# A transformer block on one Trainium2 core: the second RMS norm's root and reciprocal taken by token, four values a partition

## Chip, cores and metric

One core of a Trainium2 chip runs the whole program in one launch. The core has five engines, each with its own instruction stream: TensorE (PE in the profile, its weight loads PEld), VectorE (DVE), ScalarE (ACT), GpSimd (POOL) and SyncE (SP), which here only issues transfers. They wait for each other through semaphores. The metric is the device time of one execution in microseconds; lower is better.

## The reference, cut to what matters

Everything is float32, with 512 tokens and 1024 channels.

```python
def rms_norm(x, g):
    x32 = x.astype(jnp.float32)
    y = x32 * lax.rsqrt(jnp.mean(x32 * x32, axis=-1, keepdims=True) + EPS)
    return (y * g.astype(jnp.float32)).astype(x.dtype)
...
        mod = (cond @ w_ada[l] + b_ada[l])[:, None, :]
        shift1, scale1, gate1, shift2, scale2, gate2 = jnp.split(mod, N_MOD, axis=-1)
        n1 = rms_norm(h, g_norm1[l]) * (1 + scale1) + shift1
        z = n1 @ w_in[l]
        ...
        h = h + gate1 * (merged @ w_out[l])
        n2 = rms_norm(h, g_norm2[l]) * (1 + scale2) + shift2
        h = h + gate2 * peer(n2, w_pq[l], sub_keys[l], peer_u[l], peer_v[l])
    return rms_norm(h, g_final)
```

The change concerns `n2`, the second `rms_norm`. `peer` begins with `n2 @ w_pq`, scores against keys, and picks the best 16 of each of 8 heads for every token; its dense part runs over 16384 expert rows.

## The kernel before

Up to `peer`, activations are stored transposed: a channel is a partition and the 512 tokens lie along the row, in KT = 8 tiles of 128 channels. `hT` is the residual stream, `nT` the normed one. The program is written out by hand, engine by engine; the order in the code is the order on the engine, and semaphores tie them together.

The work around the second norm, in order:

- TensorE multiplies `w_out` with the merged branches, 8 output tiles of 24 products of 128x512 (L784).
- For each output tile d, VectorE adds it, gated, into `hT` (L1561), ScalarE squares it (`square`, L1121) into one of two buffers `sq`, and VectorE adds the squares of the tiles together in `std` (`sum_square`, L1555). `std` and `rstd` are the two halves of the tile `stats`.
- The modulation vector `mod` (six parts of 1024) is made alongside: VectorE forms `macc[q]` (L1341) and TensorE sums each over its 128 partitions by 8 products with one column each (`modulation(q)`, L621). These narrow products have a 128x128 weight load apiece. Parts 3, 4 and 5 are summed behind the `w_out` products; part 3 and 4 are shift and scale of this norm, part 5 is the last gate.
- TensorE adds `std` over the channels by one product with a matrix of ones (L793), so that every partition holds all 512 sums. ScalarE takes the root (`root`, L983), which needs a table load, VectorE the reciprocal of 128x512 values (L1319) and multiplies it into the 8 tiles (L1326), and ScalarE applies scale and shift (`modulate`, L989).
- TensorE then multiplies `n2` with `w_pq` (`pq_tile`, L630): 16 output tiles of 8 products, tile k of the first waits for `n_ready` k. Its products, as all of its type here, are in float32, which the profile shows as two records each with 128x128 weights: one product is "x2".
- Scores of a head (L825) go through ScalarE (L1166) to VectorE, which sorts out the best 16.

Since TensorE takes its instructions in order, the first `pq_tile` cannot begin before `modulation(4)` and `modulation(5)` are through.

Of the kernel before, what the change touches and what calls it, by code (L numbers as in the profile page):

```python
# [7 lines left out]
P = 128  # L8
D = 1024
T = 512  # L10
KT = D // P
TB = T // P
CT = 4
# [61 lines left out]
N_RMS1 = 0  # L75
# [5 lines left out]
N_RMS2 = N_WOUT + KT  # L81
N_PQ = N_RMS2 + 1
N_LIST = N_PQ + 2 * PH
BANKS = 4

def build(nc, stream, wada, skT, xT, cols, rows, biasd, identd, puT, pu, pv, gmat, hsave, out):
    f32, f32r, i32, u32 = mybir.dt.float32, mybir.dt.float32r, mybir.dt.int32, mybir.dt.uint32
    ALU, ACT, AX = mybir.AluOpType, mybir.ActivationFunctionType, mybir.AxisListType
    NEG = -3.0e38  # L90

    with ExitStack() as ctx:
# [3 lines left out]
        def sem(name):  # L96
            return ctx.enter_context(nc.semaphore(name))
# [15 lines left out]
        hT = big[:, 8 * D:12 * D].rearrange("p (k t) -> p k t", k=KT)  # L113
        nT = big[:, 12 * D:16 * D].rearrange("p (k t) -> p k t", k=KT)
# [4 lines left out]
        bias = low[:, 0:2 * D].rearrange("p (h k) -> p h k", k=KEYS)  # L119
# [3 lines left out]
        ident = sb("ident", [P, P])  # L123
        ones = sb("ones", [P, P])
        eps = sb("eps", [P, 1])
# [4 lines left out]
        std, rstd = stats[:, 0:T], stats[:, T:2 * T]  # L130
# [12 lines left out]
        sq = att[:, 6 * T:8 * T].rearrange("p (a t) -> p a t", a=2)  # L143
# [14 lines left out]
        zeros = sb("zeros", [P, P])  # L158
        ssum = sb("ssum", [P, TB])
        sstd = sb("sstd", [P, TB])  # L160
# [140 lines left out]
        sq_ready, sq_used = sem("sq_ready"), sem("sq_used")  # L301
        sum_ready, y_summed, lsum_ready = sem("sum_ready"), sem("y_summed"), sem("lsum_ready")
        scaled = sem("scaled")
        n_ready = sem("n_ready")
        gate_done, gate_taken = sem("gate_done"), sem("gate_taken")
        gates_ready = sem("gates_ready")
# [44 lines left out]
        def freed(eng, n):  # L351

            eng.wait_ge(bank_free[n % BANKS], n // BANKS + 1)
# [237 lines left out]
        def _(pe):  # L591
            def bank(n):

                if n >= BANKS:
                    pe.wait_ge(bank_free[n % BANKS], n // BANKS)
                return ps[:, n % BANKS, :]
# [20 lines left out]
            def modulation(q):  # L617

                pe.wait_ge(macc_ready, q + 1)
                for c in range(KT):  # L620
                    mm = nc.tensor.matmul((MOD if q < 2 else MOD2 if q == 2 else MOD3 if q < 5 else MOD5)[:, q * KT + c:q * KT + c + 1],  # L621
                                          macc[q][:, c * P:(c + 1) * P], ones[:, 0:1], start=(q >= 2),
                                          stop=(q >= 2 or (q == 1 and c == KT - 1)))
                return mm
# [130 lines left out]
            o = bank(N_LN)  # L755
# [33 lines left out]

            pe.wait_ge(attn_merged, KT)  # L790
            modulation(3)
            pe.wait_ge(sum_ready, KT - 1)
            nc.tensor.matmul(bank(N_RMS2), ones[:, :], std, start=True, stop=True).then_inc(tile_done, 1)  # L793
            modulation(4).then_inc(mod_done, 1)
            modulation(5).then_inc(mod_done, 1)

            def transposed(i, src, b, half):
# [170 lines left out]
        def _(act):  # L968
# [12 lines left out]
            def root(n, count):  # L981
                act.wait_ge(tile_done, n + 1)
                f(std, ps[:, n % BANKS, :], ACT.Sqrt, bias=eps[:, 0:1], scale=1.0 / count  # L983
                  ).then_inc(bank_free[n % BANKS], 1)
# [131 lines left out]
            def square(k):  # L1116

                freed(act, N_WOUT + k)
                if k >= 2:
                    act.wait_ge(sum_ready, max(k - 2, 1))  # L1120
                f(sq[:, k % 2, :], hT[:, k, :], ACT.Square).then_inc(sq_ready, 1)  # L1121
# [2 lines left out]
                wout_round(d)  # L1124
                square(d - 2)

            for k in range(KT - 2, KT):
                square(k)
            root(N_RMS2, D)
            act.wait_ge(mod_ready, 4)  # L1130
            modulate()

# [170 lines left out]
        def _(dve):  # L1303
# [3 lines left out]
            def step(ins):  # L1307

                count[0] += 1
                ins.then_inc(dve_step, 1)  # L1310

            def settled():

                dve.wait_ge(dve_step, count[0])

            def scale_rows(stage, between=None):
                n = N_RMS2 if stage else N_RMS1
                freed(dve, n)
                step(v.reciprocal(rstd, std))  # L1319
                settled()  # L1320
                for k in range(KT):
                    if stage and k == 0:
                        dve.wait_ge(gate_done, 2 * KT)
                    if stage and between:
                        between(k)
                    v.tensor_tensor(nT[:, k, :], hT[:, k, :], rstd, ALU.mult).then_inc(scaled, 1)  # L1326
                    if between and not stage:
                        between(k)

            def take_mod(src, c0, c1):  # L1330
                return v.tensor_tensor(mod[:, c0:c1], src[:, c0:c1], b_ada[:, c0:c1], ALU.add)
# [78 lines left out]
            for i in range(KT):  # L1410
                chunk(i)
            dve.wait_ge(x_here, 16)
            scale_rows(0, early_chunk)
            w_rest(0)
            w_rest(1)
            first_coefficients()
# [133 lines left out]
            def sum_square(k):  # L1550

                dve.wait_ge(sq_ready, KT + CT + k + 1)
                if k > 1:
                    dve.wait_ge(sum_ready, k - 1)
                v.tensor_tensor(std, sq[:, 0, :] if k == 1 else std, sq[:, k % 2, :], ALU.add).then_inc(sum_ready, 1)  # L1555

            dve.wait_ge(mod_ready, 2)
            for d in range(KT):
# [8 lines left out]
                    chunk(5 * KT - 2 + 2 * d + 1)  # L1567
                if d >= 2:
                    sum_square(d - 1)
            sum_square(KT - 1)  # L1570
            for k in range(4, KT):
                freed(dve, N_WOUT + k)
            def second_coefficients(k):
                if k == 0:
# [2 lines left out]
                    dve.wait_ge(mod_ready, 3)  # L1577
                    v.scalar_tensor_tensor(coef[:, 1, :], mod[:, 4 * KT:5 * KT], 1.0, g2, ALU.add, ALU.mult
                                           ).then_inc(mod_ready, 1)
            scale_rows(1, second_coefficients)  # L1580
            dve.wait_ge(mod_done, 4)
            step(take_mod(MOD5, 5 * KT, 6 * KT))
            settled()
# [356 lines left out]
```

## Time and profile before

| | |
|---|---|
| time, median of 3 runs | 1626.87 us (1626.63 to 1627.47) |
| time of the profiled execution | 1631.68 us |
| its span in the trace | 1629.9 us |
| mean granted clock of TensorE | 0.985 of 2.4 GHz |
| PE busy | 1589.4 us, 98% |
| DVE busy | 1375.0 us, 84% |
| ACT busy | 636.2 us, 39% |
| chain that ended last | PE 81%, DVE 12%, DMA 3% |

### The profile page before, as it was taken

Reading aid. Unit: us, or ns where it says so; the run is one execution under the profiler, and the core shown is the slowest. Engines: PE = TensorE matmul, PEld = TensorE weight load, DVE = VectorE, ACT = ScalarE, POOL = GpSimd, SP = SyncE. Lnnn points to the kernel's source line nnn. Section 1 sums busy time; section 2 is a strip of 40 time slices with the busy share of each in tenths; the row PEclk is TensorE's granted clock in tenths of the full one; section 3 lists DMA queues with packets and bytes.
Section 4 is the critical chain, followed back from the end, with each engine's and each line's share of the span. In section 5 each row is a group of like instructions: output and inputs, shape, how many; then the busy total and the mean of one; then the engine's idle time right before and its main releaser. Section 6 shows DMA issues by size and latency. Waiting matters only on the chain.

```text
span 1629.9 us, 23615 instructions
## 1 busy us (share of the span) xinstructions
PE 1589.4 (98%) x7933; PEld 1314.9 (81%) x7933; DVE 1375.0 (84%) x2751; ACT 636.2 (39%) x952; POOL 560.0 (34%) x479
## 2 busy tenths in 40 slices
PE   6999999999999999999999999999999999999997
PEld 4887764675556799988988889898889898898886
DVE  6787877764999999977989898988988888988886
ACT  3334654241112566663333333333333333333333
POOL 0000000011555300005545455554545565656520
PEclk7999999989999999999999999999999999999999
DMA  9432215641212255589999999999999999999981
GB/s 366 177 119 78 78 52 182 229 157 65 91 71 84 73 196 212 187 293 357 385 372 358 371 361 368 372 358 370 355 349 347 334 362 363 347 346 355 355 296 61
DMA packets 144459, 417.87 MB, mean 256 GB/s; under 512 B 11520, under 2 KB 56576, under 8 KB 138624
## 3 DMA queue, kind: packets, MB, share of 16 engines
q1 hardware_dynamic: 96128, 247.01, 42.2%
q0 software_dynamic: 47104, 167.83, 27.1%
q10 hardware_dynamic: 1152, 2.10, 0.3%
q8 instruction: 40, 0.66, 0.2%
q14 instruction: 35, 0.29, 0.1%
HBM read 389.59 MB, written 27.26 MB: 256 GB/s over the span
## 4 chain that ended last, share of the span: by engine, by line
PE 81%; DVE 12%; DMA 3%; issue 2%; ACT 1%; SPq 0%; DVEq 0%; ACTq 0%
PE ps L919 30%; PE ps L857 26%; PE ps L639 11%; PE ps L630 6%; PE ps L907 3%; PE ps L784 3%; DMA big<-pv 1%; DVE low L1764 1%; DVE att L1632 1%; DMA big<-wada 1%; DVE att L1643 1%; DVE big L1630 1%; DVE big L1648 1%; DVE low L1609 1%; DVE low L1757 1%
## 5 line engine op out<-in xcount | busy, mean ns | idle before, releaser
L919 PE MATMUL ps<-Vs,As 128*128 128x512 f32 x2286 | 537.1, 390 | 2.7 <-DVE As L1796 2.7
L919 PEld LDWEIGHTS ps<-Vs,As 128*128 128x128 f32 x2286 | 426.3, 188 | 87.5 <-DVE As L1796 3.0
L857 PE MATMUL ps<-xs,Us 128*128 128x352 f32 x2832 | 472.2, 322 | 2.7 <-DVE Us L1776 2.2
L857 PEld LDWEIGHTS ps<-xs,Us 128*128 128x128 f32 x2832 | 453.9, 188 | 15.8 <-DVE Us L1751 3.6
L568 POOL DMA_INDIRECT big<-pv,islot x160 | 234.3, 1465 | 167.5 <-DVE low L1835 81.8
L1275 ACT ACTIVATE att<-ps 128x352 f32<-128x352 f32 x96 | 44.7, 466 | 413.5 <-PE ps L857 413.5
L1793 DVE TENSOR_TENSOR Vs<-big,Vs 128x1024 fp32r<-128x1024 f32 x127 | 155.3, 1223 | 35.3 <-ACT Vs L1281 35.2
L630 PE MATMUL ps<-big 128*128 128x512 f32 (+1 forms) x416 | 162.8, 550 | 0.0
L1835 DVE SCALAR_TENSOR_TENSOR low<-big,act_w,low 128x1024 f32<-128x1024 f32 x128 | 157.3, 1279 | 0.0
L1281 ACT ACTIVATE Vs<-big 128x1024 fp32r<-128x1024 f32 x127 | 134.0, 1055 | 53.5 <-PE ps L919 42.4
L630 PEld LDWEIGHTS ps<-big 128*128 128x128 f32 x416 | 79.5, 194 | 74.9 <-issue 58.5
L568 POOL DMA_INDIRECT low<-pu,islot x80 | 101.4, 1268 | 101.8 <-DVE colv L1805 85.7
L516 POOL TENSOR_TENSOR xs<-big,xs 128x352 fp32r<-128x352 f32 x8 | 7.1, 928 | 361.0 <-ACT xs L1137 361.0
L1154 ACT ACTIVATE Us<-big 128x1024 fp32r<-128x1024 f32 x118 | 124.0, 1050 | 12.9 <-DMA big<-puT 12.8
L568 POOL DMA_INDIRECT big<-pu,islot x80 | 102.6, 1282 | 67.7 <-DVE colv L1805 36.9
L1790 DVE TENSOR_TENSOR att<-att 128x352 f32<-128x352 f32 x96 | 50.3, 523 | 88.8 <-ACT att L1275 87.5
L1776 DVE TENSOR_TENSOR Us<-big,Us 128x1024 fp32r<-128x1024 f32 x95 | 116.0, 1221 | 8.4 <-ACT Us L1154 8.4
L639 PE MATMUL ps<-ahi,whi 128*128 128x512 f32 x240 | 97.6, 407 | 3.3 <-DVE alo L1355 3.3
L1764 DVE TENSOR_SCALAR low<-iotan,att 128x128 f32<-128x128 f32 x352 | 97.7, 341 | 0.0
L559 POOL COPY islot<-eidx 128x8 int32 (+1 forms) x40 | 27.0, 675 | 203.1 <-DMA gmat<-big 170.5
L639 PE MATMUL ps<-alo,whi 128*128 128x512 f32 x240 | 95.3, 397 | 0.0
L639 PE MATMUL ps<-ahi,wlo 128*128 128x512 f32 x240 | 95.1, 396 | 0.0
(233 smaller groups left out, 2035.4 us busy)
## 6 DMA issues: line engine op xcount, KB each, us to landing
big<-puT SPq DMA_DIRECT2D x128, 512.0 KB, 6.0
big<-pv SPq DMA_DIRECT2D x64, 1024.0 KB, 11.2
big<-stream SPq DMA_DIRECT2D x31, 1024.0 KB, 4.9
gmat<-big SPq DMA_DIRECT2D x11, 2048.0 KB, 7.2
att<-gmat SPq DMA_DIRECT2D x31, 704.0 KB, 11.8
low<-wada SPq DMA_DIRECT2D x28, 512.0 KB, 5.2
work<-wada SPq DMA_DIRECT2D x12, 512.0 KB, 5.2
big<-wada SPq DMA_DIRECT2D x8, 512.0 KB, 13.5
```

The source lines that it names most:

```text
L568: nc.gpsimd.indirect_dma_start(out=places[r % ROWBUF], out_offset=None, in_=table, in_offset=bass.IndirectOffsetOnAxis(ap=islot[:, half, s ...
L630: mm = nc.tensor.matmul(o, lhs(k), rhs(k), start=(k == 0), stop=(k == count - 1))
L639: mm = nc.tensor.matmul(o, w, a[:, k, :], start=(k == 0 and w is hi and a is ahi), stop=(k == KT - 1 and w is lo))
L857: mm = nc.tensor.matmul(ps[:, 6 + e, 0:ET], a, xs[:, b, k, XTOK:DT], start=(k == 0 and a is hi and b == 0), stop=(k == KT - 1 and a is lo))
L919: mm = nc.tensor.matmul(ps[:, 2 * b + half, :], a, v_parts[:, w, half * T:(half + 1) * T], start=(opens and a is hi and w == 0), stop=(las ...
L1154: f(Us[:, e, 0, :], uraw[:, e, :], ACT.Copy).then_inc(uhi_ready, 1)
L1281: f(Vl[:, 0, :] if last and d == BODY - 1 else Vs[:, d % 2, 0, :], vraw[:, d // 2 % 2, d % 2, :], ACT.Copy).then_inc(vhi_ready, 1)
L1764: mm = v.tensor_scalar(ohi[:, 4 * c + t, :], iotan[:, :], lists[:, 0, tok:tok + 1], lists[:, 2, tok:tok + 1], ALU.is_equal, ALU.mult)
L1776: v.tensor_tensor(Us[:, e, 1, :], uraw[:, e, :], Us[:, e, 0, :].bitcast(f32), ALU.subtract).then_inc(ulo_ready, 1)
L1790: v.tensor_tensor(ga, ga, graw[:, (d // GRUN + 1) % 2, :, d % GRUN, :], ALU.mult).then_inc(a_ready, 1)
L1793: v.tensor_tensor(V[:, 1, :], vraw[:, d // 2 % 2, d % 2, :], V[:, 0, :].bitcast(f32), ALU.subtract).then_inc(vlo_ready, 1)
L1835: i = v.scalar_tensor_tensor(acc[:, r % 2, :], src, w, acc[:, r % 2, :], ALU.mult, ALU.add)
```

## The change

Three things are different.

1. VectorE no longer adds the last squares into `std` (`sum_square(KT - 1)` is gone). TensorE sums per token instead: the data become the weights and a column of ones the moving side, so that the sum of a token lands in the partition of that token. Four products take `std`, which holds tiles 0 to 6, four take `sq` of the last tile, one more with zeros opens the bank.
2. ScalarE takes the root of 128x4 values, after a root of `eps` alone that stands ahead of the last square, and VectorE the reciprocal of 128x4.
3. VectorE multiplies the identity matrix by those four columns into `rstd` (128x512, one diagonal per block of 128 tokens), TensorE multiplies it by ones into PSUM bank 4, and VectorE's eight multiplications read that bank instead of `rstd` in SBUF. This product stands between `modulation(4)` and `modulation(5)`.

```diff
@@ TensorE
             modulation(3)
-            pe.wait_ge(sum_ready, KT - 1)
-            nc.tensor.matmul(bank(N_RMS2), ones[:, :], std, start=True, stop=True).then_inc(tile_done, 1)
+            o = bank(N_RMS2)
+            nc.tensor.matmul(o[:, 0:TB], zeros[:, :], ones[:, 0:TB], start=True, stop=False)
+            pe.wait_ge(sum_ready, KT - 2)
+            for b in range(TB):
+                nc.tensor.matmul(o[:, b:b + 1], std[:, b * P:(b + 1) * P], ones[:, 0:1], start=False, stop=False)
+            pe.wait_ge(sq_ready, KT + CT + KT)
+            for b in range(TB):
+                mm = nc.tensor.matmul(o[:, b:b + 1], sq[:, (KT - 1) % 2, b * P:(b + 1) * P], ones[:, 0:1], start=False,
+                                      stop=(b == TB - 1))
+            mm.then_inc(tile_done, 1)
             modulation(4).then_inc(mod_done, 1)
+            pe.wait_ge(root_spread, 1)
+            nc.tensor.matmul(ps[:, 4, :], ones[:, :], rstd, start=True, stop=True).then_inc(root_done, 1)
             modulation(5).then_inc(mod_done, 1)
@@ ScalarE
-            for k in range(KT - 2, KT):
-                square(k)
-            root(N_RMS2, D)
+            square(KT - 2)
+            f(sstd[:, 0:1], eps[:, 0:1], ACT.Sqrt)
+            square(KT - 1)
+            act.wait_ge(tile_done, N_RMS2 + 1)
+            f(sstd[:, :], ps[:, N_RMS2 % BANKS, 0:TB], ACT.Sqrt, bias=eps[:, 0:1], scale=1.0 / D
+              ).then_inc(bank_free[N_RMS2 % BANKS], 1)
@@ VectorE
+            def scale_tokens(between):
+
+                freed(dve, N_RMS2)
+                step(v.reciprocal(srstd[:, :], sstd[:, :]))
+                settled()
+                v.tensor_tensor(rstd.rearrange("p (b t) -> p b t", b=TB), ident[:, :].unsqueeze(1).broadcast_to([P, TB, P]),
+                                srstd[:, :].unsqueeze(2).broadcast_to([P, TB, P]), ALU.mult).then_inc(root_spread, 1)
+                dve.wait_ge(gate_done, 2 * KT)
+                between(0)
+                dve.wait_ge(root_done, 1)
+                for k in range(KT):
+                    v.tensor_tensor(nT[:, k, :], hT[:, k, :], ps[:, 4, :], ALU.mult).then_inc(scaled, 1)
...
-            sum_square(KT - 1)
...
-            scale_rows(1, second_coefficients)
+            scale_tokens(second_coefficients)
```

TensorE's instructions behind the `w_out` products, before (the operands are named out<-in; `work` holds `macc[3]` to `macc[5]`, `stats` is `std`):

```order
L621 MATMUL ps<-ones,work 128x1 x7
L793 MATMUL ps<-stats,ones 128x512 [waits bank_free1,sum_ready]
L621 MATMUL ps<-ones,work 128x1 [waits macc_ready]
L621 MATMUL ps<-ones,work 128x1 x7
L621 MATMUL ps<-ones,work 128x1 [waits macc_ready]
L621 MATMUL ps<-ones,work 128x1 x7
L630 MATMUL ps<-big 128x512 [waits n_ready,bank_free2,w_here3]
L630 MATMUL ps<-big 128x512 [waits n_ready] x7
```

The same place in the changed kernel, whose lines are numbered anew (L631 is the `w_pq` product, `att` holds `sq`, `stats` is `std` in L797 and `rstd` in L805):

```order
L622 MATMUL ps<-ones,work 128x1 x7
L794 MATMUL ps<-ones,zeros 128x4 [waits bank_free1]
L797 MATMUL ps<-ones,stats 128x1 [waits sum_ready]
L797 MATMUL ps<-ones,stats 128x1 x3
L800 MATMUL ps<-ones,att 128x1 [waits sq_ready]
L800 MATMUL ps<-ones,att 128x1 x3
L622 MATMUL ps<-ones,work 128x1 [waits macc_ready]
L622 MATMUL ps<-ones,work 128x1 x7
L805 MATMUL ps<-stats,ones 128x512 [waits root_spread]
L622 MATMUL ps<-ones,work 128x1 [waits macc_ready]
L622 MATMUL ps<-ones,work 128x1 x7
L631 MATMUL ps<-big 128x512 [waits n_ready,bank_free2,w_here3]
```

One product of 512 columns ahead of `modulation(4)` has given way to one of four columns and eight of one, and a product of 512 columns now stands ahead of `modulation(5)`.

VectorE from the last tile's `hT` on, before:

```order
L1561 SCALAR_TENSOR_TENSOR big<-ps,mod,big 128x512 [waits tile_done]
L1555 TENSOR_TENSOR stats<-stats,att 128x512 [waits sum_ready,sq_ready] x2
L1319 RECIPROCAL stats<-stats 128x512 [waits bank_free0,bank_free3,bank_free1,bank_free2]
L1331 TENSOR_TENSOR mod<-ps,colv 128x16 [waits mod_done,gate_done,dve_step]
L1578 SCALAR_TENSOR_TENSOR coef<-mod,colv 128x8 [waits mod_ready]
L1326 TENSOR_TENSOR big<-big,stats 128x512 x8
L1331 TENSOR_TENSOR mod<-ps,colv 128x8 [waits mod_done]
```

And in the changed kernel:

```order
L1582 SCALAR_TENSOR_TENSOR big<-ps,mod,big 128x512 [waits tile_done]
L1576 TENSOR_TENSOR stats<-stats,att 128x512 [waits sum_ready,sq_ready]
L1341 RECIPROCAL srstd<-sstd 128x4 [waits bank_free0,bank_free3,bank_free1,bank_free2]
L1343 TENSOR_TENSOR stats<-ident,srstd 128x512 [waits dve_step]
L1352 TENSOR_TENSOR mod<-ps,colv 128x16 [waits mod_done,gate_done]
L1598 SCALAR_TENSOR_TENSOR coef<-mod,colv 128x8 [waits mod_ready]
L1349 TENSOR_TENSOR big<-big,ps 128x512 [waits root_done]
L1349 TENSOR_TENSOR big<-big,ps 128x512 x7
L1352 TENSOR_TENSOR mod<-ps,colv 128x8 [waits mod_done]
```

The last sum of squares and the wide reciprocal are gone, a 128x4 reciprocal and a 128x512 product with the identity have come, and the eight multiplications now stand behind `root_done` and read `ps`.

## Rows read from the trace of the kernel before

**Rows 1.** The page: span, granted clock of TensorE in 40 slices.

```profile
span 1629.9 us, 23615 instructions
...
PEclk7999999989999999999999999999999999999999
```

**Rows 2.** Chain that ended last, 340 to 400 us: start, us, what.

```profile
349.76 1.26 PE ps L793 x2
351.02 6.62 PE ps L621 x32
357.64 15.50 PE ps L630 x32
...
397.75 1.80 PE ps L825 x16
```

**Rows 3.** Timeline around the norm: start, us, engine, line, operation.

```profile
347.36 1.84 PE L621 MATMUL ps<-ones,work 128*128 128x1 f32 x16
...
348.23 1.48 DVE L1555 TENSOR_TENSOR stats<-stats,att 128x512 f32<-128x512 f32 x2
...
348.99 1.28 ACT L983 ACT_TABLE_LOAD   x1
...
350.81 6.83 PE L621 MATMUL ps<-ones,work 128*128 128x1 f32 x32
...
351.06 0.69 ACT L983 ACTIVATE stats<-ps,eps 128x512 f32<-128x512 f32 x1 [0.79 <-PE ps L793]
351.88 3.35 DVE L1319 RECIPROCAL stats<-stats 128x512 f32<-128x512 f32 x1 [2.18 <-ACT stats L983]
...
355.56 4.90 DVE L1326 TENSOR_TENSOR big<-big,stats 128x512 f32<-128x512 f32 x8
356.34 5.75 ACT L989 ACTIVATE big<-big,mod,coef 128x512 f32<-128x512 f32 x8 [4.59 <-DVE big L1326]
...
357.50 15.64 PE L630 MATMUL ps<-big 128*128 128x512 f32 x32
358.50 0.34 PEld L630 LDWEIGHTS ps<-big 128*128 128x128 f32 x1 [0.52 <-issue]
359.35 0.34 PEld L630 LDWEIGHTS ps<-big 128*128 128x128 f32 x1 [0.52 <-issue]
```

**Rows 4.** Windows: us, busy of PE, PEld, DVE, ACT, POOL; clock, DMA.

```profile
349.00:350.00 1.00, 0.44 (x3) 0.36 (x3) 0.69 (x1) 1.00 (x1) 0.00 (x0) 1.00 0.57 238
350.00:351.00 1.00, 1.00 (x4) 0.42 (x3) 0.00 (x0) 0.28 (x1) 0.00 (x0) 0.80 0.00 0
351.00:352.00 1.00, 1.00 (x8) 1.00 (x6) 0.12 (x1) 0.69 (x1) 0.00 (x0) 0.50 0.00 0
...
360.00:361.00 1.00, 1.00 (x3) 0.38 (x2) 0.96 (x5) 1.00 (x2) 0.00 (x0) 0.58 0.58 90
361.00:362.00 1.00, 1.00 (x4) 0.52 (x3) 1.00 (x7) 1.00 (x3) 0.00 (x0) 1.00 0.76 270
```

**Rows 5.** VectorE, groups by line and form: busy, mean ns.

```profile
L1757 DVE TENSOR_TENSOR low<-iotan,att 128x512 f32<-128x512 f32 x88 | 60.2, 684 | 0.7 <-PE ps L907 0.5 <-PEq L901 0.2
...
L1477 DVE TENSOR_TENSOR gates<-ps,gates 128x512 f32<-128x512 f32 x8 | 5.5, 689 | 10.3 <-PE ps L630 10.3
```

**Rows 6.** Instructions on the tile sstd: ns min/median/max, starts.

```profile
L1261 ACT ACTIVATE sstd<-ssum,eps x4: 294/294/295, 1613.4 to 1625.0; 128x1 f32<-128x1 f32 x4
L1850 DVE RECIPROCAL srstd<-sstd x4: 156/160/164, 1613.8 to 1625.4; 128x1 f32<-128x1 f32 x4
```

**Rows 7.** TensorE timeline and windows where two other wide streams begin.

```profile
40.92 0.76 PE L639 MATMUL ps<-ahi,whi 128*128 128x512 f32 x1 [3.35 <-DVE alo L1355]
...
142.86 0.79 PE L639 MATMUL ps<-ahi,whi 128*128 128x512 f32 x1
...
43.60:47.00 3.40, 3.40 (x10) 2.67 (x9) 3.30 (x7) 1.68 (x3) 0.00 (x0) 0.53 0.58 237
...
142.50:146.00 3.50, 3.50 (x12) 2.65 (x11) 3.42 (x7) 1.73 (x8) 0.00 (x0) 0.53 0.01 2
```

More of the change, by code:

```diff
@@ L303, in build @@
         scaled = sem("scaled")
+        root_spread, root_done = sem("root_spread"), sem("root_done")
         n_ready = sem("n_ready")
@@ L1314, in settled, with scale_rows @@
                 dve.wait_ge(dve_step, count[0])
-            def scale_rows(stage, between=None):
-                n = N_RMS2 if stage else N_RMS1
-                freed(dve, n)
+            def scale_rows(between):
+                freed(dve, N_RMS1)
                 step(v.reciprocal(rstd, std))
@@ L1321, in scale_rows @@
                 for k in range(KT):
[L1322 to L1325, printed above, removed]
                     v.tensor_tensor(nT[:, k, :], hT[:, k, :], rstd, ALU.mult).then_inc(scaled, 1)
-                    if between and not stage:
-                        between(k)
+                    between(k)
+            def scale_tokens(between):
[9 more added lines that the diff above has]
+                    v.tensor_tensor(nT[:, k, :], hT[:, k, :], ps[:, 4, :], ALU.mult).then_inc(scaled, 1)
             def take_mod(src, c0, c1):
@@ L1412, in _ @@
             dve.wait_ge(x_here, 16)
-            scale_rows(0, early_chunk)
+            scale_rows(early_chunk)
             w_rest(0)
```

## The prediction

> **What bounds the kernel now.** I began with the page, to see how long the span is and where TensorE's clock is below full [rows 1]. Then I took the chain that ended last around the second norm, to see who hands over to whom [rows 2], the timeline of the same stretch, to see what runs beside that chain [rows 3], and windows of 1 us, for the clock [rows 4].
>
> The chain comes out of the last sum over squares into TensorE's product with ones at 349.76 and then stays on TensorE: 32 records of L621, which are `modulation(4)` and `modulation(5)`, to 357.64, then the `w_pq` products, and so on to the scores of the second head at 397.75 [rows 2]. It does not go through the wide reciprocal. That one runs from 351.88 for 3.35 us, VectorE's multiplications begin at 355.56, and ScalarE's `modulate` at 356.34 [rows 3]. ScalarE does 8 tiles in 5.75 us, so 0.72 each, and the first normed tile is ready at 357.06. TensorE begins `w_pq` at 357.50 [rows 3]. So TensorE's own queue ends last, 0.4 us behind the norm: the norm's detour over ScalarE and VectorE lies almost wholly beside narrow products. A shorter detour alone can bring 0.4 us and no more.
>
> The second thing to see is the clock. It reads 1.00 up to 350, 0.80 in the next microsecond and 0.50 after that; the windows between 352 and 360 read 0.50 too, 360 to 361 reads 0.58, and then it is 1.00 [rows 4]. With two levels, 0.80 means a fall at 350.6 and 0.58 a rise at 360.84. It is the fall from 2.4 to 1.2 GHz, and TensorE had done narrow products since 347.36, with one wide one (512 columns) in between. It came back 3.3 us after the wide `w_pq` products began. From 357.50 to 360.84 these ran at half rate, which loses 1.67 us of work.
>
> **What the narrow and wide products cost.** At 2.4 GHz the 8 products of `modulation(3)` take 1.84 us [rows 3]; the last one's tail is in that, so I take 0.22 each. At 1.2 GHz 16 of them go from 350.81 to 357.50, 0.42 each [rows 3]. A wide float32 product is two records; at 1.2 GHz its weight loads start 0.85 us apart (358.50, 359.35), so it takes 1.70 us [rows 3], and half of that, 0.85, at 2.4 GHz.
>
> **The change, on TensorE.** Before, from the end of `modulation(3)` on: a wait, one wide product from 349.76 on, 16 narrow ones. After, behind `modulation(3)`, whose 8 products end at 347.36 + 8 x 0.22 = 349.1:
>
> - Nine narrow products (one with zeros, four on `std`, four on the last square). Their inputs are there: the first of the two last sums at 348.23 + 1.48/2 = 348.97, the last square also at about 349.0, since the table load that follows it starts at 348.99 [rows 3]. If the fall of the clock stays at 350.6, 6.8 of them run at 0.22 and 2.2 at 0.42: end at 351.5.
> - `modulation(4)`, 8 x 0.42: 354.9.
> - The spreading product, wide, at 1.2 GHz: 1.70, to 356.6. It waits for `root_spread`; see below.
> - `modulation(5)`, 3.36: 360.0.
>
> So `w_pq` can start at 360.0, against 357.50: **+2.5 us**. The removed wide product (0.85 at full clock) and the removed wait of 0.7 (349.1 to 349.76) are in this; what is added is nine narrow products, and the wide one comes back at half clock.
>
> **The change, off TensorE.** The narrow sums land some 0.3 us behind their last product, 351.8: the removed product took 1.26 us to its end [rows 2] where 0.85 is its streaming, which bounds such a tail by 0.4. A root of 128x4 is not in the trace; a root of 128x1 takes 0.294 and a reciprocal of 128x1 0.16 [rows 6]. The upper bounds are the 128x512 forms, 0.69 and 3.35 [rows 3]; four values are close to one, so I take 0.3 and 0.16, to 352.3 with 0.1 for the hand-overs. The product with the identity reads two broadcast operands; the nearest row is L1757, the same shape with broadcasts, 0.684 [rows 5]. It is ready at 353.1, and TensorE asks for it at 354.9: `modulation(4)` hides it with 1.8 us to spare. Only with the reciprocal at its upper bound would the wait show, with 1.4 us. The early table load falls into ScalarE's wait for the last tile of `hT`. It was hidden before as well: it ended at 350.27 and the root began at 351.06 [rows 3]. Its gain is nothing.
>
> From the spreading product on: it lands at 356.6 + 0.4 = 357.0. VectorE's first multiplication now reads PSUM; the nearest row, L1477, shows 0.689 for a tile with one operand in PSUM, against 4.90/8 = 0.61 for SBUF alone [rows 3, 5]. With ScalarE's 0.72 the first normed tile is ready at 358.4. TensorE is free at 360.0, so this is hidden with 1.6 us to spare; cover for it is `modulation(5)`. Tiles then come every 0.72, and TensorE needs 0.85 or 1.70 for one. VectorE's eight multiplications end 0.6 us later relative to their start, with nothing waiting. Bank 4 is read until about 362.6 and next written by the scores, behind both `pq_tile`s of the first head, more than 12 us later. What VectorE does next, diagonals for the last gate, is wanted by TensorE only behind these 16 products.
>
> **The clock behind it.** `w_pq` loses half of the time from its start to the rise. Rises in this trace: 3.3 us after the wide products began (here), 5.9 (40.92 to 46.8) and 2.9 (142.86 to 145.8); the last two by means of 0.53 over 3.4 and 3.5 us, which put 0.2 us at full clock at the window's end [rows 7]. So the loss behind 360.0 is 1.45 to 2.95 us, against 1.67 before. The whole is +2.5 - 0.2 = +2.3 to +2.5 + 1.3 = **+3.8 us**. At the same TensorE work, everything to the second head's scores follows one for one [rows 2].
>
> The profiled execution took 1631.68 us, its span 1629.9, and is 4.8 us over the median of the runs (1626.87). So its clock need not be that of the timed runs in every place, and I take a value near the lower end, +2.6, because the fall may also come later there: 1626.9 + 2.6 = **1629.5 us**, which is +0.16%. I count a difference within 0.2%, 3.25 us, as none, since measurements of this kernel hardly tell it from no change.
>
> **The rivals.**
>
> *The spreading product counts as the start of the wide stream.* It starts at 354.9, so the clock would be back 2.9 to 5.9 us later, at 357.8 to 360.8. Earliest: `modulation(5)` runs 1.2 us at half rate (2.9 products) and the rest, 5.1 x 0.22 = 1.1, at full: `w_pq` from 358.9 at full clock. The kernel before, with its loss, is as if it had started at 357.50 + 1.67 = 359.17. That is -0.3 us. Latest: start 360.0, loss 0.4, so +1.2. For it: it is the only wide work ahead of `w_pq`. Against it: the product at 349.76 did not keep the clock from falling at 350.6, and eight narrow ones follow the spreading product. Time 1626.6 to 1628.1.
>
> *The clock does not fall at all (the faster side).* In the changed kernel TensorE has no idle time from the `w_out` products to `w_pq`, where before it waited 0.7 us. At full clock: nine narrow to 351.1, `modulation(4)` 352.9, the spread just ready then (352.7 by the steps above), 353.7, `modulation(5)` 355.5; the first tile at 353.7 + 0.4 + 0.69 + 0.72 = 355.5 as well. Against 359.17 this is -3.7 us, 1623.2. It decides only if the clock holds past all of it: each microsecond longer at 2.4 GHz gives half a microsecond, so +2.6 is used up when the fall comes 5 us later, at 355.8. Against it: from 351 to 357.5 TensorE is busy without a gap, with narrow products, and the granted clock stays at 0.50 [rows 4]. The Trainium skill, "TensorE: Matmul & The Clock Gate", Part 1, has the clock gated by how busy the engine has been, idle being what throttles it; taken as the profile's busy time this would speak for this rival and for 1623.2. By the rows narrow products do not hold the clock up.
>
> *The rise comes late and the start too.* If the rise takes 5 us or more, as at 40.92, the loss is over 2.5 and the sum over +3.3: slower by more than 0.2%, 1630.2 to 1630.7. The rows allow 2.9 to 5.9; about a third of it lies there.
>
> *The wait for `root_spread` or for the multiplications from PSUM ends last.* With 1.4 us shown for the first it would be +4 and 1630.9; the rows give it 1.8 and 1.6 us of cover, so it needs prices far from the nearest rows.
>
> **How the numbers follow.** TensorE's queue with the clock falling where it does now: 0.70, of which 0.22 beyond +3.25. The spreading product helps the clock: 0.15. No fall: 0.07. A new wait, or a later low stretch that grows: 0.08, slower. Faster by over 0.2%: 0.07. Within 0.2%: 0.48 + 0.15 = 0.63. Slower: 0.22 + 0.08 = 0.30. The range leaves out the two cases with 0.07 and 0.08 and keeps the others: -0.3 to +3.8, a little wider for the timed runs, 1626.3 to 1631.2.
>
> **What would show it in the profile after.** Right: nine narrow products end near 351.5, the fall stays near 350.6, VectorE's reciprocal takes under 0.3 us and ends by 352.5, TensorE has no wait ahead of the spreading product, that one takes 1.7 us, `w_pq` starts near 360.0 and the rise follows 2.9 to 5.9 us later; the chain stays on TensorE. Wrong: a granted clock of 1.00 between 351 and 357 (then faster), `w_pq` that begins behind ScalarE instead of behind L622, or an idle TensorE ahead of L805.

## The result and the profile after

The changed kernel takes 1631.25 us at the median of 17 runs (1627.89 to 1634.50), the kernel before 1627.47 in the same measurement (17 runs, 1625.05 to 1629.54). The ratio is 1.0018 with a 95% interval of 1.0011 to 1.0026: some 2.9 us slower, clear of no change. It lies inside the 0.2% that I had set as a bound, though the interval reaches past it. (The two medians alone are 3.8 us apart; the ratio is not that of the medians.) In two later measurements, each on its own chip with experiments beside it, the changed kernel came out at 1.0008 (0.9995 to 1.0020) and 1.0011 (1.0002 to 1.0020), so +1.3 and +1.8 us. The three intervals overlap: slower is clear in two of them, each leaves the size open by a bit over 1 us to either side.

The profiled execution of the changed kernel is, of all things, shorter than that of before: its span is 1628.2 us against 1629.9 [rows 1]. The page's row of clock tenths says where to look for the reason: its first slice differs from before, ahead of anything that the change touches.

```profile
span 1628.2 us, 23650 instructions
...
PEclk8999999989999999999999999999999999999999
```

TensorE's granted clock is at 0.50 for 50.5 us of the span of before and for 43.7 us of this one. Around the norm it is low for longer now (below); the difference the other way lies in stretches far from the change (one near 142 us [rows 7] and one near 542 us are in the profile of before and not in this one). So one span says nothing about a change of 3 us. What can be compared is the stretch itself, counted from the start of `modulation(3)`: 347.36 before [rows 3], 345.45 here.

The timeline of the stretch after the change (start, us, engine, line, operation, idle time before):

```profile
345.45 1.84 PE L622 MATMUL ps<-ones,work 128*128 128x1 f32 x16
...
347.15 0.36 PE L794 MATMUL ps<-ones,zeros 128*128 128x4 f32 x2
...
347.38 1.03 PE L797 MATMUL ps<-ones,stats 128*128 128x1 f32 x8
...
348.27 1.32 PE L800 MATMUL ps<-ones,att 128*128 128x1 f32 x8
...
349.45 3.55 PE L622 MATMUL ps<-ones,work 128*128 128x1 f32 x16
349.63 0.26 ACT L1142 ACTIVATE sstd<-ps,eps 128x4 f32<-128x4 f32 x1 [2.56 <-PE ps L800]
350.02 0.18 DVE L1341 RECIPROCAL srstd<-sstd 128x4 f32<-128x4 f32 x1 [3.02 <-ACT sstd L1142]
350.23 0.69 DVE L1343 TENSOR_TENSOR stats<-ident,srstd 128x512 f32<-128x512 f32 x1
...
352.86 2.06 PE L805 MATMUL ps<-stats,ones 128*128 128x512 f32 x2
...
354.71 3.41 PE L622 MATMUL ps<-ones,work 128*128 128x1 f32 x16
...
354.96 4.87 DVE L1349 TENSOR_TENSOR big<-big,ps 128x512 f32<-128x512 f32 x8 [1.47 <-PE ps L805]
355.74 5.75 ACT L1000 ACTIVATE big<-big,mod,coef 128x512 f32<-128x512 f32 x8 [5.85 <-DVE big L1349]
...
357.98 8.50 PE L631 MATMUL ps<-big 128*128 128x512 f32 x14
```

The diagonal is written by 350.92 and TensorE takes it up at 352.86, behind `modulation(4)`. ScalarE has its first tile at 355.74 + 0.72 = 356.46, while TensorE comes to `w_pq` at 357.98, behind `modulation(5)`. The chain that ended last says the same (start, us, what):

```profile
347.52 0.89 PE ps L797 x8
348.41 1.18 PE ps L800 x8
349.59 3.41 PE ps L622 x16
353.00 1.92 PE ps L805 x2
354.92 3.20 PE ps L622 x16
358.12 16.08 PE ps L631 x32
```

Before, it came through VectorE's last sum into L793, which the row ahead of [rows 2] shows:

```profile
349.01 0.70 DVE stats L1555
```

Now, between 340 and 400 us, it never leaves TensorE. The windows show the clock (its value stands behind the five busy columns, as in [rows 4]):

```profile
348.00:349.00 1.00, 1.00 (x10) 1.00 (x10) 0.00 (x0) 0.00 (x0) 0.00 (x0) 0.93 0.00 0
349.00:350.00 1.00, 1.00 (x6) 1.00 (x6) 0.00 (x0) 0.26 (x1) 0.00 (x0) 0.50 0.00 0
...
362.00:363.00 1.00, 1.00 (x3) 0.37 (x2) 0.00 (x0) 1.00 (x4) 1.00 (x2) 0.74 0.97 410
```

It falls at 348.86 and is back at 362.5, 13.65 us later; before it was low from 350.61 to 360.85, 10.24 us.

VectorE's first maximum over the scores of the first head is a point that all versions share, behind the low clock. Here, then before:

```profile
385.80 1.64 DVE L1641 MAX8 att<-big 128x8 f32<-128x128 f32 x8 [24.12 <-ACT big L1180]
...
384.73 1.65 DVE L1621 MAX8 att<-big 128x8 f32<-128x128 f32 x8 [22.43 <-ACT big L1166]
```

That is 40.35 and 37.37 us behind the start of `modulation(3)`: **3.0 us later**. I use this distance, "to the first scores", for the experiments as well, and beside it the distance to the first `w_pq` product.

The difference is still there at the dense part, though it doesn't look so at first. Its first product starts 203.90 us behind `modulation(3)` in the changed kernel and 202.69 before, only 1.2 us apart:

```profile
542.38 4.90 PE L631 MATMUL ps<-big 128*128 128x352 f32 x16
...
549.35 2.95 PE L868 MATMUL ps<-xs,Us 128*128 128x352 f32 x17
...
541.39 6.59 PE L630 MATMUL ps<-big 128*128 128x352 f32 x16
...
550.05 2.15 PE L857 MATMUL ps<-xs,Us 128*128 128x352 f32 x12
```

The first two rows are of the changed kernel. The profile of before had the clock at 0.50 for 3.41 us from 541.75 on, and the same 16 records took 1.7 us longer there. Without that it is 2.9 us. Such a stretch stands there in the second trace of the changed kernel too and not in the third, so it doesn't go with the change.

### The profile page after: what moved, and what is told of

It is laid out like the page before. It is cut to its first block, busy times and chain, and to the rows that moved or that the text cites. A ratio compares the mean times of both kernels' runs of the same rounds, so it can differ in the third digit from the quotient of the medians.

```text
span 1628.2 us, 23650 instructions
## 1 busy us (share of the span) xinstructions
PE 1588.6 (98%) x7951; PEld 1314.4 (81%) x7951; DVE 1371.6 (84%) x2751; ACT 636.4 (39%) x953; POOL 563.4 (35%) x479
## 4 chain that ended last, share of the span: by engine, by line
PE 81%; DVE 12%; DMA 3%; issue 2%; ACT 1%; SPq 0%; DVEq 0%; ACTq 0%
PE ps L930 30%; PE ps L868 26%; PE ps L640 10%; PE ps L631 6%; PE ps L918 3%; PE ps L785 3%; DMA big<-pv 1%; DVE low L1784 1%; DVE att L1652 1%; DMA big<-wada 1%; DVE att L1663 1%; DVE big L1650 1%; DVE big L1668 1%; DVE low L1629 1%; DVE low L1777 1%
## 5 line engine op out<-in xcount | busy, mean ns | idle before, releaser
L631 PE MATMUL ps<-big 128*128 128x512 f32 (+1 forms) x416 | 161.7, 547 | 0.0
L631 PEld LDWEIGHTS ps<-big 128*128 128x128 f32 x416 | 78.9, 192 | 74.4 <-issue 57.8
## 6 DMA issues: line engine op xcount, KB each, us to landing
att<-gmat SPq DMA_DIRECT2D x31, 704.0 KB, 13.3
```

What stands on the lines that cost most here:

```text
L631: mm = nc.tensor.matmul(o, lhs(k), rhs(k), start=(k == 0), stop=(k == count - 1))
```

## The experiments

Two theories went in. Q: TensorE's queue got longer and the clock comes back later for it. N: the norm's own way over ScalarE and VectorE sets the start of `w_pq`. The last column is the timed ratio to the kernel before within one measurement; the distances, in us behind the start of `modulation(3)`, come from one trace each.

| kernel | to `w_pq` | clock at 0.50, from and to | to the first scores | ratio, 95% |
|---|---|---|---|---|
| before | 10.14 | 3.25, 13.49 | 37.37 | 1 |
| changed | 12.53 | 3.41, 17.06 | 40.35 | 1.0018 (1.0011 to 1.0026) |
| changed, 2nd time | 13.26 | 2.60, 16.26 | 40.31 | 1.0008 (0.9995 to 1.0020) |
| changed, 3rd time | 12.66 | 3.28, 16.93 | 40.35 | 1.0011 (1.0002 to 1.0020) |
| changed, 64-column modulations | 11.46 | 3.18, 10.01 | 37.02 | 0.9996 (0.9983 to 1.0009) |
| before, 64-column modulations | 9.94 | 10.34, 13.75 | 37.20 | 0.9992 (0.9980 to 1.0004) |
| the same, 2nd time | 9.95 | 10.34, 13.76 | 37.21 | 0.9999 (0.9989 to 1.0009) |
| before, last square by a second wide product | 9.94 | 8.78, 15.61 | 38.32 | 0.9992 (0.9981 to 1.0004) |
| changed, `modulation(5)` behind a `w_pq` tile | 12.21 | 2.35, 16.00 | 41.44 | 1.0026 (1.0014 to 1.0037) |
| changed, all squares added on VectorE | 11.81 | 3.35, 17.01 | 39.96 | 1.0018 (1.0007 to 1.0029) |
| before, nine one-column products more | 12.35 | 3.61, 17.26 | 40.36 | 1.0017 (1.0007 to 1.0028) |
| before, nine 64-column products more | 12.69 | 3.23, 16.88 | 40.34 | 1.0015 (1.0003 to 1.0026) |
| changed, 64 columns in all narrow products | 8.59 | none | 34.16 | 0.9980 (0.9970 to 0.9991) |
| the same, 2nd time | 8.60 | none | 34.16 | 0.9975 (0.9963 to 0.9988) |

**The changed kernel again.** No edit. Expected:

> The changed kernel once more, beside the experiments of this group. Theory Q (TensorE's queue got longer, and the clock comes back later for it): from the start of modulation(3) to the start of w_pq 12.5 us, as in its first trace, and 2 to 4 us over the kernel before in time. Theory N (the norm's own way over ScalarE and VectorE sets the start of w_pq) has w_pq begin right behind a tile of ScalarE's modulate.

> The changed kernel again, beside the two below on one chip. Over the kernel before by 0.1 to 0.25%.

The first scores came where Q has them, the time did not: 2 to 4 us over the kernel before was expected and +1.3 us measured (interval -0.8 to +3.3). In the third measurement it is +0.11%, at the low end of the expected 0.1 to 0.25%. The distances to the first scores repeat within 0.04 us. The distance to `w_pq` does not (12.5 to 13.3), since the fall of the clock comes anywhere from 2.6 to 3.4 us behind the start of `modulation(3)`; what an early fall costs ahead of `w_pq` an earlier rise gives back inside it. The medians were 1631.26 and 1630.42 us.

**64 columns in the modulations of the changed kernel.** The weights and their order stay; each product writes 64 equal columns, and VectorE reads one of them (parts 3 and 4 in two additions where it was one).

```diff
+        WIDE = {q: ps[:, b, 0:64 * KT].rearrange("p (c w) -> p c w", w=64) for q, b in ((3, 7), (4, 6), (5, 5))}
...
+                if q >= 3:
+                    for c in range(KT):
+                        mm = nc.tensor.matmul(WIDE[q][:, c, :], macc[q][:, c * P:(c + 1) * P], ones[:, 0:64],
+                                              start=True, stop=True)
+                    return mm
```

> The changed kernel, with the products of modulation(3) to modulation(5) made 64 columns wide instead of one (the same weights, all columns alike, one of them read). Work on the weights is the same. Theory Q with the clock as part of the cause: if wider products hold the granted clock at 1.00, the nine narrow products, two modulations and the spreading product take 2.0 + 1.8 + 0.85 + 1.8 us, w_pq starts 8.2 to 8.6 us behind modulation(3) and at full clock, 4 to 6 us faster than the changed kernel and 1 to 3 us faster than the kernel before. Rival (the clock follows something else, such as waits): clock falls all the same, time within 1 us of the changed kernel. Theory N: no gain, since the norm's way is not touched.

The clock still fell, at 347.84 with the nine one-column products, but it was back at 354.67, ahead of `w_pq`, instead of inside it. The rows of the timeline and of a window:

```profile
348.87 3.65 PE L624 MATMUL ps<-ones,work 128*128 128x64 f32 x16
...
354.13 2.15 PE L624 MATMUL ps<-ones,work 128*128 128x64 f32 x16
...
354.00:355.00 1.00, 1.00 (x7) 0.86 (x6) 0.62 (x2) 0.00 (x0) 0.00 (x0) 0.66 0.00 0
```

`modulation(4)` still takes 3.65 us and `modulation(5)` 2.15. The first scores come 3.3 us earlier than in the changed kernel, 37.02, and 0.35 us earlier than before. The timed ratio went from 1.0008 to 0.9996, which is 2 us where I had put down 4 to 6; the two intervals overlap. Against the kernel before, where I had put down 1 to 3 us, there is no measurable gain. The expectation was too high, since I had the clock held throughout. N has no place for the earlier scores at all.

**The same in the kernel before.**

> The kernel before with the same 64-column modulations. Theory Q: if the clock holds, modulation(4) and (5) end early and the norm's way with the wide reciprocal becomes the bound: w_pq starts about 9.7 us behind modulation(3)'s start (10.1 before), at full clock instead of half, so 1.5 to 2.5 us faster than before, less than the changed kernel gains. If the clock falls during the wait for the norm instead, then no gain. Theory N: the gain is equal in both kernels or none.

> The kernel before with 64-column modulations, again. 0.9985 to 1.0000 of the kernel before: the wide reciprocal bounds it once the modulations are quick.

Here both modulations end early (32 records in 3.68 us, where it was 6.83 [rows 3]), and for once `w_pq` waits for ScalarE:

```profile
348.61 3.68 PE L623 MATMUL ps<-ones,work 128*128 128x64 f32 x32
...
355.19 15.67 PE L636 MATMUL ps<-big 128*128 128x512 f32 x32 [2.90 <-ACT big L995]
```

It begins only 0.2 us sooner than before, and 0.4 us behind its start, after the wait of 2.90 us, the clock falls (355.59, to 359.00). So `w_pq` loses 1.7 us to the low clock, as before. Time 0.9992 and 0.9999, no measurable change: the wait took back what the quick modulations gave. That the wait made the clock fall is likely from the order of events and was not tested.

**The last square by a second wide product, in the kernel before.**

```diff
+            o = bank(N_RMS2)
+            pe.wait_ge(sum_ready, KT - 2)
+            nc.tensor.matmul(o, ones[:, :], std, start=True, stop=False)
+            pe.wait_ge(sq_ready, KT + CT + KT)
+            nc.tensor.matmul(o, ones[:, :], sq[:, (KT - 1) % 2, :], start=False, stop=True).then_inc(tile_done, 1)
```

`sum_square(KT - 1)` is gone with it.

> One part of the change alone: the last square is summed on TensorE, but by a second product of 512 columns into the same bank; root, reciprocal and multiplications are as before. Theory Q: one wide product (0.85 us) more and a wait of 0.7 us less in TensorE's queue, w_pq at 10.1 to 10.4 us behind modulation(3)'s start, time within 0.7 us of before. If the second wide product holds the clock longer, 1 to 2 us faster. Theory N (VectorE's sum out of the way by 0.7 us matters): 0.5 to 0.7 us faster by that alone.

With two wide products the fall came at 353.87, 8.78 us behind the start of `modulation(3)` instead of 3.25, although the modulations kept their one column. The modulations took 3.63 us, and `w_pq` again waited for ScalarE, from 355.03 on. The low stretch then lay on `w_pq` for 5.7 us, so the first scores came 0.95 us later than before, 38.32. A longer hold had been named as possible, and it came; the 1 to 2 us that I had hung on it did not. The time shows no change, 0.9992 with an interval over 1, so the part "last squares on TensorE" costs at most some 0.7 us in this form (the interval's upper end, 1.0004). The trace has it slower and the ratio has it faster; the sign is open.

**`modulation(5)` behind the first `w_pq` tile, in the changed kernel.**

```diff
-            modulation(5).then_inc(mod_done, 1)
...
                 pq_tile(w, 0)
+                if w == 0:
+                    modulation(5).then_inc(mod_done, 1)
```

> The changed kernel with modulation(5) moved behind the first w_pq tile. Theory Q: TensorE reaches w_pq at once behind the spreading product and now waits for the norm; w_pq starts 1.4 to 1.6 us earlier, 11.0 us behind modulation(3)'s start; modulation(5) costs 1.7 us at full clock inside w_pq, or 3.4 at half. The first scores reach VectorE 0 to 2 us earlier than in the changed kernel, depending on when the clock rises. Theory N (norm's way bounds anyway): w_pq starts no earlier.

A miss. I had `w_pq` at 11.0, and it came at 12.21: the clock fell at 2.35, the spreading product started at 8.38 where it was 7.41 in the first trace of the changed kernel, and the norm's way came behind that. `w_pq` did wait for the norm, and so began 3.8 us behind the spreading product's start, where it was 5.1:

```profile
352.62 2.05 PE L805 MATMUL ps<-stats,ones 128*128 128x512 f32 x2
...
356.45 8.99 PE L631 MATMUL ps<-big 128*128 128x512 f32 x16 [1.78 <-ACT big L1001]
...
365.27 1.84 PE L622 MATMUL ps<-ones,work 128*128 128x1 f32 x16
```

But TensorE stood idle for 1.78 us, the clock came back no sooner (16.0 us behind `modulation(3)`, as in the second trace of the changed kernel), and `modulation(5)` then cost 1.7 us at full clock on the path. The first scores came 1.1 us later than in the changed kernel, and the ratio is the highest of all, 1.0026, though its interval overlaps that of the changed kernel.

**All squares added on VectorE, in the changed kernel.** Four narrow products less; `sum_square(KT - 1)` is back and the four products on `sq` are gone.

> The changed kernel with all squares added on VectorE as before, so TensorE has five narrow products instead of nine. Theory Q: four narrow products less (0.9 us at full clock), one wait of 0.5 to 0.7 us for VectorE's last sum: w_pq starts 12.0 to 12.5 us behind modulation(3), time within 0.7 us of the changed kernel. Theory N: VectorE's sum is back in the norm's way and w_pq starts 0.7 us later.

TensorE waited 0.33 us for VectorE's last sum, where I had 0.5 to 0.7, and `w_pq` began at 11.81, a little ahead of the expected 12.0 to 12.5 and earlier than in any trace of the changed kernel. First scores 0.4 us earlier, time the same (1.0018). N had `w_pq` 0.7 us later.

**Nine products of zeros in the kernel before.** Nothing else of the change.

```diff
+            for b in range(9):
+                nc.tensor.matmul(ps[:, 6, b:b + 1], zeros[:, :], ones[:, 0:1], start=True, stop=True)
             pe.wait_ge(sum_ready, KT - 1)
             nc.tensor.matmul(bank(N_RMS2), ones[:, :], std, start=True, stop=True).then_inc(tile_done, 1)
```

> The kernel before with nine one-column products of zeros ahead of its product with ones, and nothing else: the price of the added narrow products alone. They fill the wait of 0.7 us and run 1.3 us past it. Theory Q: w_pq starts 11.2 to 11.6 us behind modulation(3)'s start (10.1 before), 1 to 2 us slower. Theory N: the norm's way has 0.4 us of slack only, so also 0.9 us slower, but with w_pq starting behind ScalarE's modulate and not behind L621.

This alone makes the changed kernel's loss: 40.36 against 40.35 to the first scores. In time it is 1.0017, where the changed kernel had 1.0008 to 1.0018 in other measurements. `w_pq` has no wait ahead of it and starts 0.45 us behind the first normed tile (ScalarE starts on it at 356.60 and takes 0.72, so 357.32). So N's version, a start right behind ScalarE, is not seen. It began 1 us later than I had put down, because the product with ones now stands behind the fall of the clock and runs at half rate:

```profile
347.12 2.25 PE L793 MATMUL ps<-ones,zeros 128*128 128x1 f32 x18
...
349.23 2.06 PE L795 MATMUL ps<-stats,ones 128*128 128x512 f32 x2
351.08 6.83 PE L621 MATMUL ps<-ones,work 128*128 128x1 f32 x32
...
357.77 16.41 PE L630 MATMUL ps<-big 128*128 128x512 f32 x32
```

**The same nine with 64 columns.** `ones[:, 0:64]` as the moving side, eight ranges of bank 6.

> The kernel before with nine products of zeros ahead of its product with ones, now 64 columns wide; modulations keep one column. Against the nine of one column this tells the queue's length from the clock. Theory Q, queue alone: w_pq starts 12.3 us behind modulation(3), as with one column, and the time is 1.001 to 1.003. Theory Q with the clock: the fall comes one step later, the product with ones runs at full clock, w_pq starts 10.8 to 11.5 us behind modulation(3)'s start and the time is 0.9995 to 1.001.

This was to tell the queue from the clock, and did not. With `modulation(3)` ahead and 16 more narrow products behind at one column, the clock fell at 3.23 all the same, and everything was as with nine narrow ones, 40.34 and 1.0015. "The fall comes one step later" was wrong.

**64 columns in all narrow products of the changed kernel.** The modulations as above, and the sums over squares too; the product with zeros covers the 256 columns.

```diff
-            nc.tensor.matmul(o[:, 0:TB], zeros[:, :], ones[:, 0:TB], start=True, stop=False)
+            nc.tensor.matmul(o[:, 0:TB * 64], zeros[:, :], gates[:, 4:5, 0:TB * 64].rearrange("p a t -> p (a t)"), start=True, stop=False)
...
-                nc.tensor.matmul(o[:, b:b + 1], std[:, b * P:(b + 1) * P], ones[:, 0:1], start=False, stop=False)
+                nc.tensor.matmul(o[:, b * 64:(b + 1) * 64], std[:, b * P:(b + 1) * P], ones[:, 0:64], start=False, stop=False)
```

> The changed kernel with 64 columns in all narrow products, those of the sums too, so that no stretch of one-column products is left. Theory Q with the clock: the granted clock stays at 1.00 from the w_out products into w_pq, which starts 8.3 to 8.8 us behind modulation(3)'s start at full clock; first scores at VectorE about 35.5 us behind modulation(3)'s start against 37.4 in the kernel before and 40.3 in the changed one; 1 to 2.5 us faster than the kernel before. Rival (64 columns do not count, the earlier rise in the experiment with wide modulations came from the spreading product): clock falls about 3 us behind the w_out products as before and the time is within 1 us of that experiment.

> The changed kernel with 64 columns in all narrow products, again. 0.997 to 0.999 of the kernel before, and 1 to 3 us under the kernel before with 64-column modulations: with the clock held, the narrow root and reciprocal do bring their part.

The granted clock stays at 1.00 from the `w_out` products into `w_pq`. Timeline, then two windows:

```profile
345.86 0.65 PE L800 MATMUL ps<-gates,zeros 128*128 128x256 f32 x2
346.35 1.00 PE L803 MATMUL ps<-ones,stats 128*128 128x64 f32 x8
347.19 1.06 PE L806 MATMUL ps<-ones,att 128*128 128x64 f32 x8
348.08 1.95 PE L624 MATMUL ps<-ones,work 128*128 128x64 f32 x16
...
349.87 1.08 PE L811 MATMUL ps<-stats,ones 128*128 128x512 f32 x2
350.78 1.89 PE L624 MATMUL ps<-ones,work 128*128 128x64 f32 x16
...
352.72 13.97 PE L637 MATMUL ps<-big 128*128 128x512 f32 x32
...
348.00:350.00 2.00, 2.00 (x20) 2.00 (x19) 0.87 (x2) 0.26 (x1) 0.00 (x0) 1.00 0.00 0
350.00:352.00 2.00, 2.00 (x15) 1.52 (x14) 1.43 (x5) 0.23 (x1) 0.00 (x0) 1.00 0.00 0
```

A product with 64 columns costs nearly what one with one column does at the same clock (8 in 1.89 to 1.95 us against 1.84), and each stage that stood behind the fall takes about half: the second modulation 1.95 for 3.55 us, the spreading product 1.08 for 2.06. `w_pq` starts at 8.59, the first scores come at 34.16, 6.2 us ahead of the changed kernel and 3.2 ahead of the kernel before. Timed 0.9980 and 0.9975: this version beats both kernels, at 1625.72 and 1624.70 us with 1627.88 and 1628.50 for the kernel before. The gain is larger than I had put down: scores at 34.16 for 35.5, some 3.3 and 4.1 us under the kernel before for 1 to 2.5, and, by medians, 3.5 us under the kernel before with 64-column modulations for 1 to 3.

## Why the prediction came out

The forecast was no change beyond 0.2%, slower within it: 1629.5 us or +2.6 us, up to +3.8. The measured ratio, +0.18%, is +2.9 us. The median of 1631.25 itself lies a hair above the range (1631.2), because the kernel before was at 1627.47 in that measurement and at 1626.87 when the range was made.

- **What bounds it.** That the norm's way has no more than 0.4 us to give, and TensorE's queue sets the start of `w_pq`, held. The chain after stays on TensorE, the first tile waits 1.5 us for it (forecast 1.6). The nine added products alone, in the kernel before, give the whole 3.0 us to the first scores. Theory N fell with that, and with the experiment in which VectorE's sum came back and `w_pq` came earlier.
- **TensorE's steps.** Counted from `modulation(3)`, forecast and measured: end of the nine 4.1 and 4.0, start of the spreading product 7.5 and 7.4, of `modulation(5)` 9.2 and 9.3, of `w_pq` 12.6 and 12.5. The difference to before is +2.4, forecast +2.5.
- **Off TensorE.** Root 0.26 us (0.3), reciprocal 0.18 (0.16), diagonal 0.69 (0.684), with 1.9 us of cover (1.8). The eight multiplications from PSUM take 4.87 us against 4.90 from SBUF [rows 3]: I had charged 0.6 us for PSUM, hidden in any case, and no cost shows. The charge came from a wrong reading: 0.689 is how long one instruction's record lasts, 0.61 is the spacing of eight. Like with like, the record of one multiplication lasts 0.68 us from SBUF and 0.68 from PSUM, and both start 0.60 us apart.
- **The clock.** It rose 4.5 us behind the start of `w_pq`, inside the 2.9 to 5.9 that I took from other rises. That loses 2.27 us against 1.67, so +0.6. With +2.4 this makes the 3.0 us seen to the first scores. It was the sum of the trace, +2.3 to +3.8, that this confirms; the +2.6 was a choice within it.
- **The rivals.** That the spreading product brings the clock back early did not happen in any of three traces with one-column modulations: the clock rose at 16.3 to 17.1 us behind `modulation(3)`, well inside `w_pq`. With 64-column modulations around it, it did rise early (10.01); which of the two did it was not separated. That the clock does not fall happened only in the kernel with 64 columns throughout, and its price was about right: I had -3.7 us against before, the trace shows -3.2 and the timing -0.20% and -0.25%. The Trainium skill, "TensorE: Matmul & The Clock Gate", Part 1, ties the granted clock to how busy TensorE has been. The traces agree if "busy" isn't the profile's busy share: in the changed kernel the engine was busy without a gap from 349 to 362.5 us and had 0.50 up to there, with 64 columns it was as busy up to `w_pq` (all but 0.05 us from 343 to 355) and had 1.00. Where the two readings differ, the measurement decides.

Two things in it were luck. The timed +2.9 us is the largest of three; +1.3 and +1.8 us are in the range too, but would have made +2.6 look high. And the working takes the fall at 3.3 us behind `modulation(3)` as given. In the second trace it came at 2.6. The distance to the first scores did not move, but that these two effects cancel was not foreseen.

What stays open: what share of the gain of the 64-column version belongs to the narrow root and what to the clock. Against the kernel before with 64-column modulations it is 3.0 us earlier at the first scores (34.16 and 37.20), of which 1.35 us is an earlier `w_pq` and the rest, 1.7, half of the 3.4 us low stretch which that kernel falls into just behind its wait. A kernel before whose clock is held past that wait was not run. Open as well is why the timed difference was smaller in the two later measurements than the 3.0 us that all three traces show to the first scores.

## What to carry to other kernels

Before a detour over two engines is shortened, look at what the waiting engine does meanwhile: here its queue of products ended 0.4 us behind the detour, and with the clock as it was, that was all there was to win. Work added to that queue, however small a product, counts in full once the queue's idle time is used up, and if it stands where TensorE's clock is about to fall, also pushes wide work behind it to half rate. Where a run of one-column products has to stand on the path, try 64 columns of the same: here 8 products took 0.05 to 0.11 us longer by it at the same clock. Do it for the whole run, since nine wider products amid 24 of one column changed nothing, and all 33 kept the clock.

## What the runs showed that I had not expected

- Nine one-column products of zeros, 2 us at full clock in a queue with 0.7 us of idle time, cost 2.8 us timed (1.0017) and 3.0 to the first scores, since they shift one wide product and 16 narrow ones against the clock's fall.
- Nine 64-column products amid one-column ones changed nothing (fall at 3.23 us, 1.0015), 64 columns in all 33 narrow products held the clock altogether. With 24 of the 33 wider, the fall stayed (3.18) and the rise came earlier (10.01 for 17.06). In the kernel before, where all 24 narrow products were made wider, the fall came only behind TensorE's wait for the norm (10.34). More columns are not the only thing that moved it: a second product of 512 columns among one-column ones did so too (8.78 for 3.25).
- Executions of one kernel differ in where else the clock is low: three profiles of the changed kernel have it at 0.50 for 43.7, 48.3 and 53.5 us of the span, with spans of 1628.2, 1627.1 and 1633.3. A timed median moves by less, but a single span can show the wrong sign, as the first pair here does.
